# Attention scores of a two-layer encoder: plain float32 matmuls from q and k in place of three products of two-part copies

## What is computed

```python
s = jnp.einsum('bhqd,bhkd->bhqk', q * HEAD_DIM ** -0.5, k) + bias   # HEAD_DIM = 64
pr = jax.nn.softmax(s, axis=-1)
o = jnp.einsum('bhqk,bhkd->bhqd', pr, v)
```

## Time and profile before

| | |
|---|---|
| median of three runs | 1279.23 us (1278.7 to 1279.29) |
| span of the profiled execution, first to last instruction | 1277.9 us |
| median above that span | 1.3 us |
| PE busy | 1269.3 us, 99% |
| DVE busy | 866.6 us, 68% |
| ACT busy | 683.5 us, 53% |
| mean granted TensorE clock | 0.999 |
| mixer loops | about 297 to 403 us and 929 to 1040 us of the span |

### The profile page before, as it was taken

One profiled execution on the slowest core, in us unless ns is written; L12 is line 12 of the kernel. 1 busy time (PEld: TensorE's weight loads), 2 busy tenths in 40 slices (PEclk: granted clock), 3 DMA queues, 4 the chain that ended last, 5 costly groups with the idle time before them and its releaser, 6 DMA issues.

```text
span 1277.9 us, 17739 instructions
## 1 busy us (share of the span) xinstructions
PE 1269.3 (99%) x6827; PEld 1084.1 (85%) x6827; DVE 866.6 (68%) x1244; ACT 683.5 (53%) x936; POOL 40.7 (3%) x59
## 2 busy tenths in 40 slices
PE   9999999999999999999999999999999999999997
PEld 7888888888888888888888888888888888888886
DVE  6576667656888775566675666765578887655665
ACT  7454555445766455444554444554477653645444
POOL 0311100000000000000000000000000000000000
PEclk9999999999999999999999999999999999999999
DMA  8698855574645545555455555465556355455551
GB/s 282 224 289 252 252 201 194 198 230 149 214 122 188 185 165 197 192 180 186 175 187 197 197 192 181 156 222 187 184 184 218 124 179 184 181 197 197 197 187 44
DMA packets 59214, 245.08 MB, mean 192 GB/s; under 512 B 21344, under 2 KB 27616, under 8 KB 32408
## 3 DMA queue, kind: packets, MB, share of 16 engines
q1 hardware_dynamic: 58144, 242.54, 54.6%
q10 hardware_dynamic: 984, 1.80, 0.4%
q0 software_dynamic: 32, 0.02, 0.0%
HBM read 239.07 MB, written 5.27 MB: 191 GB/s over the span
## 4 chain that ended last, share of the span: by engine, by line
PE 97%; DMA 1%; POOL 1%; issue 0%; ACT 0%; DVE 0%; SPq 0%; POOLq 0%; DVEq 0%; ACTq 0%
PE bank L756 29%; PE bank L723 16%; PE bank L725 16%; PE bank L724 16%; PE bank L760 15%; PE bank L1066 2%; PE bank L814 1%; PE bank L821 1%; PE bank L1080 1%; DMA raw<-in_stream 1%; PE bank L986 0%; DMA gate<-in_lam 0%; POOL lam_exp L403 0%; POOL bias L424 0%; ACT whi L460 0%
## 5 line engine op out<-in xcount | busy, mean ns | idle before, releaser
L1181 DVE TENSOR_TENSOR wlo<-raw,whi 128x2048 fp32r<-128x2048 f32 x209 | 479.1, 2294 | 274.9 <-ACT whi L460 270.6
L460 ACT ACTIVATE whi<-raw 128x2048 fp32r<-128x2048 f32 x206 | 393.4, 1912 | 229.5 <-PE bank L760 139.9
L756 PE MATMUL bank<-xT,whi 128*128 128x512 f32 x1664 | 414.8, 391 | 0.0
L756 PEld LDWEIGHTS bank<-xT,whi 128*128 128x128 f32 x1664 | 301.8, 188 | 55.3 <-issue 0.5
L760 PEld LDWEIGHTS bank<-xT,wlo 128*128 128x128 f32 x1664 | 220.2, 190 | 12.8
L760 PE MATMUL bank<-xT,wlo 128*128 128x256 f32 x1664 | 224.1, 282 | 0.0
L723 PE MATMUL bank<-whi,xT 128*128 128x512 f32 x432 | 171.6, 397 | 0.0
L725 PE MATMUL bank<-whi,xT 128*128 128x512 f32 x432 | 168.5, 390 | 0.0
L724 PE MATMUL bank<-wlo,xT 128*128 128x512 f32 x432 | 168.4, 390 | 0.0
L723 PE MATMUL bank<-whi,hTh 128*128 128x512 f32 x320 | 124.8, 390 | 0.4 <-DVE hTl L1223 0.4
L724 PE MATMUL bank<-wlo,hTh 128*128 128x512 f32 x320 | 124.5, 389 | 0.0
(11 more groups left out here) (169 smaller groups left out, 1140.2 us busy)
## 6 DMA issues: line engine op xcount, KB each, us to landing
raw<-in_stream SPq DMA_DIRECT2D x209, 1024.0 KB, 4.8
bias<-t_rows SPq DMA_DIRECT2D x24, 256.0 KB, 6.5
bias<-in_rpb SPq DMA_DIRECT2D x16, 256.0 KB, 7.8
masked<-bias SPq DMA_DIRECT2D x8, 512.0 KB, 6.9
bias<-masked SPq DMA_DIRECT2D x8, 512.0 KB, 4.6
raw<-in_stream SPq DMA_DIRECT2D x10, 256.0 KB, 6.5
x<-in_x SPq DMA_DIRECT2D x4, 256.0 KB, 5.0
raw<-in_stream ACTq DMA_DIRECT2D x2, 256.0 KB, 4.0
```

Of the source, the lines that this page charges most:

```text
L460: act.activation(whi[:, s, :], raw[:, s, :], ACT.Copy).then_inc(hi_ready, 1)
L756: return pe.matmul(dst[blk][:, :], whi[:, s, w], xT[:, 4 * a + k, :, :].rearrange("p a s -> p (a s)"), start=start, stop=stop)
L1181: dve.tensor_tensor(wlo[:, s, :], raw[:, s, :], whi[:, s, :].bitcast(F32), ALU.subtract).then_inc(unit_split, 1)
```

## The change

Each score product becomes one plain float32 matmul of q against k straight from `qkT`. `pair_to_hi`, `pair_to_lo`, the names `pairh` and `pairl` and the semaphores `pair_hi` and `pair_split` go, and with them the wait of PE on `pair_split` and that of ACT on `scores_ready`.

```diff
-            def pair_to_hi(l, s):
-                if s % 4 == 0:
-                    act.wait_ge(qk_ready, l * 12 + s + 4)
-                if s:
-                    act.wait_ge(scores_ready, l * 24 + 2 * s)
-                act.activation(pairh[:, :, :], qkT[:, s // 4, :, s % 4, :], ACT.Copy).then_inc(pair_hi, 1)
...
-                    if j < PAIRS - 1:
-                        pair_to_hi(l, j + 1)
...
                 def scores(s):
                     b = s // 4
-                    pe.wait_ge(pair_split, l * 12 + s + 1)
                     if s == 0:
                         pe.wait_ge(qk_ready, l * 12 + 12)
...
-                            dst = bank[2 + m][:, t * S:(t + 1) * S]
-                            cols = slice(t * P, (t + 1) * P)
-                            last = three(dst, pairh[rows, 0, cols], pairl[rows, 0, cols], pairh[rows, 1, :], pairl[rows, 1, :],
-                                         True, True)
+                            last = pe.matmul(bank[2 + m][:, t * S:(t + 1) * S], qkT[rows, b, 0, s % 4, t * P:(t + 1) * P],
+                                             qkT[rows, b, 1, s % 4, :], start=True, stop=True)
...
-                def pair_to_lo(s):
-                    dve.wait_ge(pair_hi, l * 12 + s + 1)
-                    dve.tensor_tensor(pairl[:, :, :], qkT[:, s // 4, :, s % 4, :], pairh[:, :, :].bitcast(F32),
-                                      ALU.subtract).then_inc(pair_split, 1)
...
-                    if j < PAIRS - 1:
-                        pair_to_lo(j + 1)
```

More of the change, by code:

```diff
@@ L125, in build @@
         qkT = sb("qkT", [P, 3, 2, BLK, S])
-        pairh, pairl = hTh_last, hTl_last
         merged = qkT[:, BC, :, :, :].rearrange("p a b s -> p a (b s)")
@@ L188, in build @@
                   "pv_done", "o_turned", "t5_product", "y_done", "row_product"))
-        hi_ready, quarter_hi, squared, silu_done, h_hi, v_out, gate_ready, exp_done, pT_hi, v_hi, o_hi, pair_hi = map(
+        hi_ready, quarter_hi, squared, silu_done, h_hi, v_out, gate_ready, exp_done, pT_hi, v_hi, o_hi = map(
             sem, ("hi_ready", "quarter_hi", "squared", "silu_done", "h_hi", "v_out", "gate_ready", "exp_done",
-                  "pT_hi", "v_hi", "o_hi", "pair_hi"))
-        (unit_split, quarter_ready, quarter_scaled, quarter_split, meansq_ready, pair_split, diag_ready, row_ready, gated, h_split, qk_ready, biased,
+                  "pT_hi", "v_hi", "o_hi"))
+        (unit_split, quarter_ready, quarter_scaled, quarter_split, meansq_ready, diag_ready, row_ready, gated, h_split, qk_ready, biased,
          rden_ready, mixed, normed, pT_split, v_split, o_ready, a_squared, a_mean, a_normed, o_split, branch_read,
          t5_biased, a_premix, branch_added) = map(
-            sem, ("unit_split", "quarter_ready", "quarter_scaled", "quarter_split", "meansq_ready", "pair_split", "diag_ready", "row_ready", "gated",
+            sem, ("unit_split", "quarter_ready", "quarter_scaled", "quarter_split", "meansq_ready", "diag_ready", "row_ready", "gated",
                   "h_split", "qk_ready", "biased", "rden_ready", "mixed", "normed", "pT_split", "v_split", "o_ready", "a_squared", "a_mean",
@@ L646, in _ @@
                 act.wait_ge(t5_stored, 16)
-                pair_to_hi(l, 0)
                 for b in (1, 2):
@@ L1375, in _ @@
                 branch(0, first=True)
-                pair_to_lo(0)
                 for b in (1, 2):
```

## The result

The changed kernel takes 1282.61 us, the median of eight runs (1282.3 to 1283.51), beside 1279.09 us for the kernel before, also of eight (1278.7 to 1279.38). The ratio is 1.0027 with a 95% interval of 1.0018 to 1.0036: slower by 3.5 us. The profiled execution is the slowest of the eight, 1283.51 us, with a span of 1281.7 us.

What follows compares the result with a forecast made beforehand. PE's own work was taken to bound the kernel. Scores add 4.1 us to 1279.2, edges, ACT and DVE relief, waits and slower steps nothing: 1283.3 us, range 1281.6 to 1289.2.

Steps and rivals of the forecast that it cites:

- PE never waits: Mixer loop: its time is PE's own work, with no wait of PE on another engine; only changes on PE count.
- (1) The scores: PE's score matmuls: four steps of 0.220 us for six of 0.118, +0.17 us a call, +4.1 us over 24 calls.
- (2) The edges: PE entering and leaving the 64-row scores: 0.21 us inside and 0.09 ahead, unchanged, counted as nothing.
- The rival that lost a third of them with fewer loads: Score edges: fewer queued weight loads return 2.7 us, slower steps up to 1 us; 1279.6 to 1280.6 us; no-change chance 0.08.
- (3) to (5) ACT, DVE and the waits: Copies and waits gone, less traffic: ACT loses 15.1 us, DVE 16.5; no time gained, PE's slower steps taken as 0.
- Row groups one after the other: Plain score matmuls hold the whole array: eight steps of 0.220, +1.05 us a call, 1304.4 us; chance 0.09.
- Strict order with neighbours: Score matmuls overlap only the next one of another row group: five steps, +0.39 us a call, 1288.6 us; chance 0.07.
- The faster rival: Plain score records on 64 rows step at 0.118 us: 0.24 us less a call, -5.7 us, 1273.5 us; chance 0.04.

Runs made afterwards that it cites:

- the kept copies: Kernel before with the plain float32 score matmuls of the change, but the two-part copies on ACT and DVE and all their waits kept: 1282.87 us.
- DVE's doubled work: Kernel before with DVE's subtraction of the pair done twice, the second waiting for the first: 1279.76 us.
- the 128-row run: Changed kernel with every score matmul on all 128 rows, each summing over both heads, so run for its time only: 1294.59 us.
- the reordered kernels: All score matmuls of row group 0 put ahead of group 1: changed kernel 1282.63 us, kernel before 1287.19 us; kernel before with five and five first 1283.89 us.
- the combined kernel: The change plus plain float32 values of branches B and C, two heads side by side on 64 columns each: 1276.17 us, ratio 0.9976 to the kernel before.

## Why the prediction was right

The forecast was 1283.3 us, +4.1, in a range of 1281.6 to 1289.2; measured were 1282.61, +3.5. The mechanism is the one forecast: four steps of a plain record on PE in place of six of F32R, edges unchanged, and next to nothing for the relief.

- **The bound.** PE was the bound, and what changed on PE decided: shown by the kept copies (+3.5 us with no relief) and by DVE's doubled work (none that can be told, 0.47 us in the trace). "PE never waits" was slightly wrong, by one loss a layer behind `add_branch`, which the change removed. It stood in the earlier trace rows, as 0.16 of the 1.6 us of the weight loads put down to issue, and the text took that for no wait. The sum of an iteration in the prediction was made for the iterations of branches B and C, and the loss lies in one of branch A's first.
- **(1) The scores.** Forecast +0.17 us a call from four steps of 0.220; measured +0.15 from four of 0.2155, 3.6 us in all. The record was mis-sized by 2%, as I built it from 0.112 for 128 columns plus 0.108. The lower bound, 0.216, which has nothing fixed in it, was the better value. As the difference of two nearly equal numbers is what counts (0.88 or 0.86 against 0.71), 2% of the record became a tenth of the result. The estimate with the gap per matmul of the Trainium skill (TensorE: Matmul & The Clock Gate, Back-to-back issue gap), 5.0 us, was further off, since that formula gives 0.109 us for 256 columns and the trace has F32R at 0.118.
- **(2) The edges** stayed as they were, and the 128-row run shows that they are the change from 128 rows to 64 and back. The rival that lost a third of them with fewer loads is out.
- **(3) to (5) ACT, DVE and the waits.** The relief is worth about 0.1 us in place of 0. Another 0.3 us of iteration 9's loss went because PE's longer scores bring it there later, a term that the prediction did not have. Both errors, this one and the record's, lie on the same side, so no cancelling made the forecast good. PE's slower steps after the transposes stayed.
- **The rivals.** Row groups one after the other: the 128-row run gives its price, 1.73 us a call, and the twos in the timeline exclude it here. Strict order with neighbours: excluded by the reordered kernels. What the Trainium skill says (TensorE: Matmul & The Clock Gate, Part 3), that matmuls start strictly in order, does not hold in these traces for matmuls of different row groups. Group 1 overtakes at most four load-and-multiply pairs of group 0; within a group the order is kept. The faster rival, a plain record at F32R's step, is out: 0.2155 against 0.118.

## What to carry to other kernels

Where one engine's chain is the bound from end to end, count that engine's steps for the new and the old form, and leave the relief of the others at nothing unless a row shows a wait. Look at the waits put down to issue as well: one of PE's for DVE stood there. A plain float32 matmul costs two records of about 216 ns for 256 columns, against three F32R ones of 118 ns: plain loses to three products of parts by a fifth if the shape is the same, and wins where it lets two 64-wide halves of the array work side by side that were padded before. When two heads share the array by halves, issue them in turn, at most four load-and-multiply pairs apart.

## What I had not expected of the hardware

- Matmuls on the other row group overtake: with six F32R matmuls of group 0 ahead, group 1 started beside the third (7.9 us lost in 24 calls); with five, beside the second (4.6 us); with four records ahead nothing was lost. A group that starts late pays a step more, its first record being 0.38 us long.
- Column groups run side by side as row groups do: eight plain records of 64 columns by 256 in 1.08 us.
- Going from 128 rows to 64 and back costs about 0.34 us a call (by the run on 128 rows). Going from 64 columns to 64 rows costs about what the entry from 128 rows does (1.02 us from the first value record to the first score, of which 0.86 are four steps, and the combined kernel's iteration is the sum of both edits).
